# One transformer layer with experts: the last expert tile kept on chip and added with a marking matrix, the row array cleared during attention, tile 18 finished before tile 19 starts

## The chip, the core and the metric

The kernel runs on one core of one Trainium2 chip. The metric is the device time of one execution in microseconds (us); lower is better. PE is the matrix engine (TensorE), DVE is VectorE, ACT is ScalarE, POOL is GpSimd, and SP only issues transfers (DMAs). These engines run independently and wait for one another by semaphores. PE writes its results into PSUM, 8 banks of 128 x 512 float32; the rest of the on-chip data lies in SBUF.

## What is computed

A hybrid attention part adds to the residual x (1024 tokens of width 1024, all float32). The part that matters here is what follows it: each token picks one group of experts, and two experts in that group. The results of the two experts are weighted and added.

```python
top_v, top_i = lax.top_k(e_logits, EXPERT_TOPK)          # two experts of a token
top_w = jax.nn.softmax(top_v, axis=-1) * p_g
gates = jnp.sum(jax.nn.one_hot(eid, N_EXPERTS) * top_w[..., None], axis=1)
for e in range(N_EXPERTS):
    hid = jax.nn.silu(jnp.dot(h, w_gate[e])) * jnp.dot(h, w_up[e])
    y = y + gates[:, e:e + 1] * jnp.dot(hid, w_down[e])
x = x + gate_m[:, None] * y
return rms_norm(x, g_final)
```

## The kernel before

**Expert tiles.** Each of the 2048 (token, choice) pairs gets a slot in one of 20 tiles (NSTEP) of 128 slots. A tile is made of four chunks of 32 slots; a chunk belongs to one expert. The weights of the 32 experts stream through six on-chip places (the ring: gate and up projection together, and down projection), 3 MB for each expert. The loads are issued by SP in the order of use, each as soon as PE has finished with the place.

**Work on a tile n.** POOL gathers the 128 rows of the tile from DRAM (`gather`); PE transposes them (`turn_rows`), ACT and DVE copy them out with a scale and shift (`ev_t`); PE multiplies with gate and up weights (`gate_up`); ACT takes the sigmoid (`ev_sg`), DVE forms the hidden values (`ev_hid`); PE transposes them (`turn_hidden`), ACT copies (`ev_h`); PE multiplies with the down weights (`down_proj`); DVE multiplies by a row gate (`ev_y`) and writes `ysb`; POOL scatters the rows of `ysb` to `y_dram` in DRAM ("expert_rows", 2048 rows: row 1024 k + token for choice k). In the PE program tile n+1's `gate_up` and tile n+2's `turn_rows` stand between `turn_hidden(n)` and `down_proj(n)`. The indices of a tile's rows are in `lst` (tokens) and `dst_rows` (rows of `y_dram`), one column for each tile.

**The tail.** The residual of token tiles 0 to 5 (`x2_dram`) is read back into `XT` when tile 17 is through (L572). When all 20 scatters have landed (`rows_out`), SP reads `y_dram` back as 16 transfers of 512 KB into `yg[t][k]`, in the order of the token tiles t = 0 to 7 (L597). The four even token tiles (`mixed`) are summed by PE in PSUM: `add_into` adds the residual with the identity matrix as the stationary operand, and then y1 and y2 with diagonal matrices of the two weights (`diag`, made by ACT). The four odd ones are summed by DVE (`combine`). For each token tile ACT squares and sums (L1000), POOL takes the power -1/2 (L635, L636), DVE scales (`finish`, L1552), SP stores (L600). The order on DVE is combine(1), finish(0), combine(3), finish(1), finish(2), combine(5), finish(3), finish(4), finish(5), combine(7), finish(6), finish(7).

**Attention.** SP's last transfers before attention are those of the router weights (L504, L505); its next ones wait until the last scores are multiplied (`qk_done`, L507). `wuk` holds a weight of the key projection; PE reads it last in the `KV` steps, counted by `kv_ps`. Later `pick` (the chosen experts, one-hot) lies in the same place. POOL selects the keys (L675 to L677) and then takes the powers for the attention output (`o_scale`).

Of the kernel before, what the change touches and what calls it, by code (L numbers as in the profile page):

```python
# [64 lines left out]
def hybrid_layer(nc, x, c, w_ada, b_ada, g_attn, w_in, g_kv, w_uk, w_uv, lam_q1, lam_k1, lam_q2, lam_k2,  # L65
# [77 lines left out]
    y_dram = nc.dram_tensor("expert_rows", [2 * S, D], F32, kind="Internal").ap()  # L143

    ctx = ExitStack()
    with ctx:
# [165 lines left out]
        out_row_in, modc_set = sem("out_row_in"), sem("modc_set")  # L312
# [61 lines left out]
        yg = [[QKV[:, D * (2 * i + k):D * (2 * i + k + 1)] for k in range(2)] for i in range(T)]  # L374
# [44 lines left out]
        x2_out, x2_back = sem("x2_out"), sem("x2_back")  # L419
# [5 lines left out]
        def uses(b):  # L425

            return len(range(b, NSTEP, 2))

# [9 lines left out]
        def _(sp):  # L438
# [66 lines left out]
            sp.dma_start(wgr[:, :, NG:NR], w_router[0].rearrange("(j p) n -> p j n", p=P)).then_inc(wgr_in, 16)  # L505
            sp.wait_ge(qk_done, NA)
# [54 lines left out]
            for n in range(NSTEP + 1):  # L561
                if n < NSTEP:
                    sp.wait_ge(gu_ps, n + 1)
                    for w in freed(n):
                        gate_up_load(sp, expert_of(w), w % RING)
# [39 lines left out]
        def _(pool):  # L605
# [64 lines left out]
            for i, t in enumerate(sel_tiles):  # L670
# [30 lines left out]
            def overflow_rows(n, i, b):  # L701
# [16 lines left out]
                pool.wait_ge(y_out[ob], i * 16 + 16 * (uses(ob) + 1))  # L718
# [21 lines left out]
            for b in range(2):  # L740
                pool.wait_ge(y_out[b], 16 * uses(b))
# [7 lines left out]
        def _(act):  # L749
# [192 lines left out]
            act.wait_ge(modc_set, 1)  # L942
# [47 lines left out]
            for t in range(T):  # L990
                if t in mixed:
                    i = mixed.index(t)
                    act.wait_ge(mix_ps, i + 1)
                    whole = PS[:, 2 * i:2 * i + 2, :].rearrange("p a n -> p (a n)")
# [9 lines left out]
        def _(dve):  # L1004
# [246 lines left out]
            for i in range(NA):  # L1251
# [11 lines left out]
                if 5 <= i < NA // 2 + 2 and i % 4 == 1:  # L1263
# [17 lines left out]
                                     op1=ALU.mult).then_inc(modc_set, 1)  # L1281
# [93 lines left out]
            def order_experts():  # L1375
# [12 lines left out]
                dve.wait_ge(tables_set, 2 * NE)  # L1388
# [7 lines left out]
            for t in range(T + 1):  # L1396
# [22 lines left out]
                if t >= 1:  # L1419
                    if t == 1:  # L1420
                        dve.wait_ge(wgr_ready, 2)
# [68 lines left out]

            def ev_y(e, b, stored):
# [18 lines left out]
            dve.wait_ge(modc_set, 1)  # L1510
# [5 lines left out]
            for n in range(NSTEP):  # L1516
# [557 lines left out]
```

## Time and profile before

| what | us |
|---|---|
| median of three runs | 1051.61 |
| lowest and highest | 1050.21, 1052.73 |
| the profiled execution | 1047.62 |
| its span, first to last instruction | 1045.8 |
| PE busy in it | 952.2 (91%) |

The profiled execution is one of its own, 4.0 us below the median. Times within a profile are counted from the start of its span. A group of the profile is one line of the program and one kind of operation; "idle before" names what ended the wait of that engine. A float32 matmul of the program stands in the profile as two records of PE, so the 24 of `add_into` are 48 records.

### The profile page before, as it was taken

To read this page: it belongs to the slowest core of one execution; us is meant where nothing else is said; L and a number is where in the kernel's file an instruction comes from. 1 tells how busy PE (TensorE), PEld (TensorE's weight loads), DVE (VectorE), ACT (ScalarE), POOL (GpSimd) and SP (SyncE) were. 2 spreads that over 40 slices of the span, in tenths; PEclk is the share of its full clock that TensorE was granted. 3 is DMA by queue.
4 is the path that set the end of the run, shared out by engine and by line. 5 is a ranking of instruction groups with operands and counts; after the bars stand their busy time and mean duration, and the time that the engine had idled before them with its cause. 6 is when DMAs were issued, how large, how long until landed. Compare 5 with 4: busy or idle time off the path is not lost.

```text
span 1045.8 us, 14947 instructions
## 1 busy us (share of the span) xinstructions
PE 952.2 (91%) x5302; PEld 513.1 (49%) x5302; DVE 595.3 (57%) x1593; ACT 403.9 (39%) x909; POOL 115.7 (11%) x218
## 2 busy tenths in 40 slices
PE   3899999999999798879999899999499999979974
PEld 2463675444449476546666545556233434323421
DVE  3479548999997687777676333456333222312217
ACT  6130236666620577767668412122121111211113
POOL 3000000000038001110000000000111111111003
PEclk9999999999999999989999999999599999999989
DMA  9996101101111000040000411166899999999979
GB/s 326 331 359 228 41 22 41 41 21 40 40 30 18 1 1 1 1 173 11 1 2 2 161 61 60 61 261 248 323 418 422 419 417 422 419 421 421 397 284 377
DMA packets 69916, 191.44 MB, mean 183 GB/s; under 512 B 10248, under 2 KB 36160, under 8 KB 57552
## 3 DMA queue, kind: packets, MB, share of 16 engines
q1 hardware_dynamic: 61856, 172.63, 43.1%
q0 software_dynamic: 5760, 16.78, 4.1%
q10 hardware_dynamic: 2224, 1.05, 0.4%
q8 instruction: 43, 0.70, 0.3%
q14 instruction: 33, 0.27, 0.1%
HBM read 172.60 MB, written 22.04 MB: 186 GB/s over the span
## 4 chain that ended last, share of the span: by engine, by line
PE 79%; DMA 6%; issue 4%; DVE 4%; ACT 3%; SPq 3%; POOL 0%; POOLq 0%; ACTq 0%; DVEq 0%
PE PS L1675 16%; PE PS L1976 12%; PE PS L1861 11%; PE PS L1778 6%; PE PS L1999 6%; PE PS L1799 4%; PE PS L1821 3%; DMA SC<-in_w_up_dram 3%; PE PS L1722 3%; PE PS L1684 3%; PE PS L1816 3%; SPq L450 2%; PE PS L1963 2%; PE PS L1699 2%; PE PS L1664 1%
## 5 line engine op out<-in xcount | busy, mean ns | idle before, releaser
L1675 PE MATMUL PS<-HT,X 128*128 128x512 f32 x384 | 168.8, 593 | 0.0
L1976 PE MATMUL PS<-QKV,HT 128*32 128x512 f32 (+2 forms) x640 | 130.4, 607 | 3.4 <-DMA SC<-in_w_up_dram 1.7
L860 ACT ACTIVATE X<-X,nmx 128x896 f32<-128x896 f32 (+7 forms) x128 | 98.6, 772 | 68.5 <-DVE nmx L1205 68.0
L1675 PEld LDWEIGHTS PS<-HT,X 128*128 128x128 f32 x384 | 72.5, 190 | 92.4 <-issue 92.2
L1861 PE MATMUL PS<-QKV,HT 128*128 128x512 f32 x256 | 115.3, 604 | 0.0
L1141 DVE TENSOR_SCALAR_CACHE_REDUCE BIAS<-SC,tk 128x384 f32<-128x384 f32 (+3 forms) x128 | 96.4, 809 | 1.1
L1487 DVE TENSOR_TENSOR HT<-PS,HT 128x256 f32<-128x256 f32 x20 | 8.5, 425 | 153.3 <-ACT HT L958 153.3
L1778 PE MATMUL PS<-QKV 64*128 64x512 f32 (+3 forms) x384 | 82.1, 533 | 10.8 <-DVE nmx L1205 10.0
L837 ACT ACTIVATE X<-SC,tk 128x896 f32<-128x896 f32 x64 | 69.6, 1087 | 43.1 <-DVE tk L1129 43.1
L1861 PEld LDWEIGHTS PS<-QKV,HT 128*128 128x128 f32 x256 | 48.0, 193 | 54.6 <-issue 54.5
L1999 PE MATMUL PS<-QKV,HT 128*32 128x512 f32 (+2 forms) x320 | 65.4, 595 | 2.2 <-DMA X<-in_w_down_dram 2.2
L1205 DVE CUSTOM_DVE_ANT_0 X<-PS,R 128x256 f32<-128x256 f32 (+7 forms) x80 | 51.0, 675 | 28.6 <-PE PS L1778 28.2
L1799 PE MATMUL PS<-ident,X 128*128 128x128 f32 x432 | 66.1, 284 | 0.0
L1976 PE MATMUL PS<-SC,HT 128*32 128x512 f32 (+2 forms) x144 | 57.8, 604 | 6.3 <-issue 6.3
L958 ACT ACTIVATE HT<-PS 128x256 f32<-128x256 f32 x20 | 7.7, 384 | 143.3 <-PE PS L1976 143.3
L1976 PEld LDWEIGHTS PS<-QKV,HT 128*32 128x32 f32 (+2 forms) x640 | 38.1, 120 | 49.0 <-issue 46.2
L1976 PE MATMUL PS<-X,HT 128*32 128x512 f32 (+2 forms) x160 | 58.4, 621 | 0.8 <-DVE HT L1506 0.8
L1205 DVE CUSTOM_DVE_ANT_0 X<-PS,SC 128x1024 f32<-128x1024 f32 (+5 forms) x48 | 42.0, 887 | 29.4 <-PE PS L1778 29.4
L1799 PEld LDWEIGHTS PS<-ident,X 128*128 128x128 f32 x432 | 48.5, 143 | 10.6 <-issue 9.1
L1816 PE MATMUL PS<-QKV,HT 128*128 128x128 f32 x288 | 41.8, 291 | 11.1 <-ACT HT L870 11.0
L1778 PEld LDWEIGHTS PS<-QKV 64*128 64x128 f32 x384 | 32.5, 189 | 39.2 <-issue 25.2
L1821 PE MATMUL PS<-QKV 128*64 128x128 f32 x576 | 46.7, 285 | 4.1 <-ACT QKV L870 2.8
(295 smaller groups left out, 1462.9 us busy)
## 6 DMA issues: line engine op xcount, KB each, us to landing
QKV<-in_w_gate_dram SPq DMA_DIRECT2D x22, 1024.0 KB, 16.4
QKV<-in_w_up_dram SPq DMA_DIRECT2D x22, 1024.0 KB, 22.9
QKV<-in_w_down_dram SPq DMA_DIRECT2D x22, 1024.0 KB, 28.2
QKV<-in_w_ada_dram SPq DMA_DIRECT2D x8, 2048.0 KB, 15.5
QKV<-in_w_ada_dram SPq DMA_DIRECT2D x8, 1024.0 KB, 12.6
X<-in_w_in_dram SPq DMA_DIRECT2D x16, 512.0 KB, 3.8
QKV<-expert_rows SPq DMA_DIRECT2D x16, 512.0 KB, 10.0
X<-in_w_gate_dram SPq DMA_DIRECT2D x5, 1024.0 KB, 16.5
```

What stands on the lines that cost most here:

```text
L837: act.activation(RL[:, n % 2, 0:w], SC[:, sc_off[t]:sc_off[t] + w], ACT.Sign, bias=tk[:, 4, i:i + 1].bitcast(F32), scale=-1.0, accum_out=c ...
L860: act.activation(sc, sc, ACT.Exp, bias=nmx[:, i % 4, m:m + 1], scale=-1.0, accum_out=rs[:, i, m:m + 1]).then_inc(exp_done, 1)
L1141: dve.tensor_scalar(BIAS[:, i % 3, 0:w], SC[:, sc_off[t]:sc_off[t] + w], thr.bitcast(F32)[:, i:i + 1], 0.0, ALU.is_lt, ALU.add, accum_out= ...
L1205: dve.tensor_tensor_reduce(sc_buf[i % 4][:, m, 0:w], PS[:, 2 * m:2 * m + 2, :].rearrange("p a n -> p (a n)")[:, BANK * n:BANK * n + w], aw ...
L1675: end = pe.matmul(PS[:, 2 * b + half, :], WS[:, b, j, :], HT[:, j, BANK * half:BANK * (half + 1)], start=(j == 0), stop=(j == KC - 1))
L1778: end = pe.matmul(PS[:, 2 * m + n + c0 // BANK, 0:c1 - c0], QKV[rows_m, q0:q0 + P], QKV[rows_m, k0 + c0:k0 + c1], start=True, stop=True)
L1799: end = pe.transpose(PS[:, 4 + g % 2, c0:c0 + P], sc_buf[i % 4][:, m, P * b:P * (b + 1)], ident[:, :])
L1816: end = pe.matmul(PS[:, 6 + h % 2, slot], turned_at(i)[:, g % 4, P * (b - b0):P * (b - b0 + 1)], vf[:, u * S + P * b:u * S + P * (b + 1)], ...
L1821: end = pe.matmul(PS[DH * m:DH * (m + 1), 6 + h % 2, slot], vd[:, b, v0:v0 + DH], turned_at(i)[:, g % 4, c0:c0 + P], start=(b == 0), stop= ...
L1861: end = pe.matmul(PS[:, n % 4, :], HT[:, k, P * (n // 2):P * (n // 2 + 1)], wo[:, k, BANK * (n % 2):BANK * (n % 2 + 1)], start=(k == 0), s ...
L1976: end = pe.matmul(PS[at, 2 + b, :], hgT[b][:, P * c_ + at.start:P * c_ + at.stop], WGU[w][:, c_, :, :], start=(c_ == 0), stop=(c_ == KC - 1))
L1999: end = pe.matmul(PS[at, 5 + h, :], hidT[b][:, P * c_ + at.start:P * c_ + at.stop], WDN[w][:, c_, BANK * h:BANK * (h + 1)], start=(c_ == 0 ...
```

## The change

- **Last tile stays on chip.** Tile 19 (LAST) is no longer scattered. DVE multiplies its PSUM result by the row gate and by the weight of each row and leaves it in SBUF (`y_last`, `ev_y_last`). The weights of the rows come from DRAM: ACT stores the two weight arrays (`w_dram`, at tile 2), DVE works out the places of the 128 rows (`find_last_rows`, at tile 4), and POOL gathers them (`w_row`).
- **Marking matrix.** `mark_last_rows` builds, for each of the 8 token tiles, a 128 x 128 matrix of zeros and ones that says which token each row of tile 19 belongs to (`belongs`). PE multiplies it with `y_last`, and so adds the rows of tile 19 into PSUM for all 8 token tiles. For this the residual of all 8 goes through PE too (`begin`). For odd token tiles DVE's `combine` starts from PSUM. The even ones get y1 and y2 by diagonal matrices, as before (`mix`).
- **Cleared array.** Rows of tile 19 are no longer written to `y_dram`, so it is zeroed once: POOL clears `wuk` after the key selection, and SP writes it 32 times (256 KB each) to `y_dram` during attention.
- **Order.** For tile 18, PE runs `down_proj(18)` ahead of `gate_up(19)`; DVE runs `ev_y(18)` ahead of `ev_hid(19)`. `rows_out` now counts 19 scatters. The places of `yg` are moved, so that the reads of token tiles 0 to 2 go where tile 18's weights were; the reads of 3 to 7 wait for tile 19's last matmul.
- The semaphore `modc_set` becomes a step of `wgr_ready`; the other counts follow.

```diff
+            sp.wait_ge(tables_set, 2 * NE + 1)
+            for r in range(2 * T):
+                for h in range(2):
+                    sp.dma_start(y_dram[P * r:P * (r + 1), BANK * h:BANK * (h + 1)],
+                                 wuk[:, :, :].rearrange("p h d -> p (h d)")).then_inc(small_in, 16)
             sp.wait_ge(qk_done, NA)
...
             sp.wait_ge(rows_out, 1)
             for t in range(T):
+                if t == 3:
+                    sp.wait_ge(dn_ps, 2 * NSTEP)
                 for k in range(2):
...
+            pool.wait_ge(kv_ps, KV)
+            pool.memset(wuk[:, :, :], 0.0).then_inc(tables_set, 1)
             for h in range(NA // 8):
                 o_scale(h)
...
-                scatter(n)
+                if n < LAST:
+                    scatter(n)
+                if n == 4:
+                    pool.wait_ge(act_in, 48)
+                    pool.indirect_dma_start(out=w_row, out_offset=None, in_=w_dram,
...
+                if n == 2:
+                    act.dma_start(w_dram.rearrange("(p k t) o -> p k (t o)", k=2, t=T), rt[:, 5:7, :]).then_inc(act_in, 16)
...
+            def mark_last_rows():
+
+                link(dve.tensor_copy(tok_last, lst[:, LAST:NSTEP]))
+                link(dve.tensor_scalar(shift, first_tok[:, 0:T], tok_last, None, ALU.subtract))
+                for t in range(T):
+                    end = dve.tensor_scalar(belongs[:, P * t:P * (t + 1)], iota_p[:, :], shift[:, t:t + 1], 0.0, ALU.add,
+                                            ALU.is_equal)
+                end.then_inc(diag_done, 1)
+
+            def ev_y_last():
+
+                dve.wait_ge(w_in, 16)
+                for h in range(2):
+                    part = slice(BANK * h, BANK * (h + 1))
+                    dve.wait_ge(dn_ps, 2 * LAST + h + 1)
+                    dve.scalar_tensor_tensor(out=y_last[:, part], in0=PS[:, 5 + h, :], scalar=w_row, in1=out_row[:, part],
+                                             op0=ALU.mult, op1=ALU.mult).then_inc(y_sb, 1)
...
             for n in range(NSTEP):
                 turn_hidden(n, n % 2)
+                if n == LAST - 1:
+                    down_proj(n, n % 2, *weights_of(n))
                 if n + 1 < NSTEP:
                     gate_up(n + 1, (n + 1) % 2, *weights_of(n + 1))
                 if n + 2 < NSTEP:
                     turn_rows(n + 2, n % 2, 16 * (n // 2 + 2))
-                down_proj(n, n % 2, *weights_of(n))
+                if n != LAST - 1:
+                    down_proj(n, n % 2, *weights_of(n))
...
+            def begin(t):
+
+                add_into(t, ident[:, :], XT[:, t, :], True, False)
+                end = add_into(t, belongs[:, P * t:P * (t + 1)], y_last, False, t not in mixed)
+                if t not in mixed:
+                    end.then_inc(mix_ps, 1)
+
+            def mix(t):
+
+                i = mixed.index(t)
+                pe.wait_ge(yg_in[t], 32)
+                add_into(t, diag[:, i, 0, :], yg[t][0], False, False)
+                add_into(t, diag[:, i, 1, :], yg[t][1], False, True).then_inc(mix_ps, 1)
+
             pe.wait_ge(x2_back, 16 * SPILLED)
-            for i, t in enumerate(mixed):
-                if i == 2:
-                    pe.wait_ge(rows_out, 1)
-                add_into(i, ident[:, :], XT[:, t, :], True, False)
-            pe.wait_ge(diag_done, 8)
-            for i, t in enumerate(mixed):
-                pe.wait_ge(yg_in[t], 32)
-                add_into(i, diag[:, i, 0, :], yg[t][0], False, False)
-                add_into(i, diag[:, i, 1, :], yg[t][1], False, True).then_inc(mix_ps, 1)
+            pe.wait_ge(y_sb, 2 * NSTEP)
+            pe.wait_ge(diag_done, 9)
+            pe.wait_ge(rows_out, 1)
+            for t in range(4):
+                begin(t)
+            mix(0)
+            mix(2)
+            pe.wait_ge(fin_done, 1)
+            begin(4)
+            pe.wait_ge(cb_done, 1)
+            begin(5)
+            mix(4)
+            pe.wait_ge(fin_done, 3)
+            begin(6)
+            pe.wait_ge(cb_done, 2)
+            begin(7)
+            mix(6)
```

PE's program at its end, before. The rows are matmuls of the program ("x8" is eight in a row); `X,ident` adds the residual, and `QKV` alone stands for y1 and y2 with the diagonals.

```order
L2037 MATMUL PS<-X,ident 128x512 x8
L2037 MATMUL PS<-QKV 128x512 x16
```

After. `QKV` is here the marking matrix with `y_last` (two for each token tile), or y1 and y2 with the diagonals (four for each even token tile).

```order
L2098 MATMUL PS<-X,ident 128x512 x2
L2098 MATMUL PS<-QKV 128x512 x2
L2098 MATMUL PS<-X,ident 128x512 x2
L2098 MATMUL PS<-QKV 128x512 x2
L2098 MATMUL PS<-X,ident 128x512 x2
L2098 MATMUL PS<-QKV 128x512 x2
L2098 MATMUL PS<-X,ident 128x512 x2
L2098 MATMUL PS<-QKV 128x512 x10
L2098 MATMUL PS<-X,ident 128x512 x2
L2098 MATMUL PS<-QKV 128x512 x2
L2098 MATMUL PS<-X,ident 128x512 x2
L2098 MATMUL PS<-QKV 128x512 x6
```

Four more rows of the same kind follow (for token tiles 6 and 7: 2, 2, 2 and 6). The 24 matmuls have become 48: 16 with the identity, 16 with the marking matrix, 16 with the diagonals.

PE's program around tile 18, before: the transposes of tile 18's hidden values (`ident,HT`), the last of `gate_up(19)` (32-row chunks with the place `SC` among them), and then `down_proj(18)` (the row of x4).

```order
L1985 MATMUL PS<-ident,HT 128x128 x2
L1976 MATMUL PS<-SC,HT 32x512
L1976 MATMUL PS<-QKV,HT 32x512 x3
...
L1976 MATMUL PS<-SC,HT 32x512
L1976 MATMUL PS<-QKV,HT 32x512 x3
L1999 MATMUL PS<-QKV,HT 128x512 x4
L1985 MATMUL PS<-ident,HT 128x128 x2
```

After:

```order
L2043 MATMUL PS<-ident,HT 128x128 x2
L2057 MATMUL PS<-QKV,HT 128x512 x4
L2034 MATMUL PS<-SC,HT 32x512
L2034 MATMUL PS<-QKV,HT 32x512 x3
...
L2034 MATMUL PS<-SC,HT 32x512
L2034 MATMUL PS<-QKV,HT 32x512 x3
L2043 MATMUL PS<-ident,HT 128x128 x2
```

`down_proj(18)` has moved from behind the whole of `gate_up(19)` to ahead of it; the transposes of tile 19's hidden values now follow `gate_up(19)` directly.

## Rows read from the trace of the kernel before

**Rows 1.** Chain that ended last, 985 us on: start us, duration us, what.
```profile
988.27 7.07 PE PS L1976 x64
995.34 3.63 PE PS L1999 x8
...
999.67 3.69 PE PS L1999 x32
...
1003.38 0.70 DVE HT L1497
...
1004.85 5.75 DMA expert_rows<-HT,dst_rows
...
1016.02 10.62 DMA QKV<-expert_rows
```

**Rows 2.** Groups by form, 1003 to 1046 us: busy us, mean ns | idle before, releaser.
```profile
L2037 PE MATMUL PS<-QKV 128*128 128x512 f32 x32 | 14.4, 599 | 2.8 <-DMA QKV<-expert_rows 2.8
L2037 PE MATMUL PS<-X,ident 128*128 128x512 f32 x16 | 9.0, 728 | 6.1 <-DMA X<-residual_rows 6.1
```

**Rows 3.** Timeline of the end: start us, us, engine, line, operation [idle before <-releaser].
```profile
1021.90 1.02 ACT L1000 ACTIVATE HT<-PS 128x1024 f32<-128x1024 f32 x1 [18.89 <-PE PS L2037]
...
1023.98 1.28 DVE L1552 SCALAR_TENSOR_TENSOR X<-PS,ss,BIAS 128x1024 f32<-128x1024 f32 x1 [2.26 <-POOL ss L636]
...
1031.80 3.70 PE L2037 MATMUL PS<-QKV 128*128 128x512 f32 x8 [1.42 <-DMA QKV<-expert_rows]
1032.34 0.19 PEld L2037 LDWEIGHTS PS<-QKV 128*128 128x128 f32 x1 [0.24 <-issue]
...
1032.77 0.19 PEld L2037 LDWEIGHTS PS<-QKV 128*128 128x128 f32 x1 [0.24 <-issue]
...
1035.54 1.02 ACT L1000 ACTIVATE HT<-PS 128x1024 f32<-128x1024 f32 x1 [1.66 <-PE PS L2037]
...
1037.02 1.39 POOL L636 TENSOR_TENSOR ss<-ss,neghalf 128x1 f32<-128x1 f32 x1
...
1041.45 1.28 DVE L1552 SCALAR_TENSOR_TENSOR X<-X,ss,BIAS 128x1024 f32<-128x1024 f32 x1 [0.93 <-POOL ss L636]
```

**Rows 4.** Load of tile 18's down weights, issued 961.4: time to landing.
```profile
L414 SPq DMA_DIRECT2D QKV<-in_w_down_dram x1: 1645/1645/1645, 961.4 to 961.4; - x1
...
DMA to landing us min/median/max: 29.2/29.2/29.2
```

**Rows 5.** Timeline at tile 18's hidden values and behind them.
```profile
987.11 0.50 PE L1985 MATMUL PS<-ident,HT 128*128 128x128 f32 x2
...
987.31 2.98 SPq L572 DMA_DIRECT2D X<-residual_rows  x6
987.65 0.38 ACT L964 ACTIVATE HT<-PS 128x256 f32<-128x256 f32 x1 [2.50 <-PE PS L1985]
...
996.27 0.42 DVE L1489 TENSOR_TENSOR HT<-HT,PS 128x256 f32<-128x256 f32 x1
...
998.81 0.39 PE L1985 MATMUL PS<-ident,HT 128*128 128x128 f32 x2
```

**Rows 6.** Start of the tail: scatter of tile 19, first residual matmul, first read.
```profile
1009.40 9.03 PE L2037 MATMUL PS<-X,ident 128*128 128x512 f32 x16 [6.09 <-DMA X<-residual_rows]
...
1010.65 9.83 SPq L597 DMA_DIRECT2D QKV<-expert_rows  x16
```

**Rows 7.** Windows: us; busy of PE, PEld, DVE, ACT, POOL; PE clock; DMA share; GB/s.
```profile
1018.00:1022.00 4.00, 4.00 (x10) 1.69 (x10) 2.57 (x2) 0.10 (x1) 0.00 (x0) 1.00 1.03 413
...
1008.00:1012.00 4.00, 2.60 (x3) 1.18 (x4) 0.00 (x0) 0.00 (x0) 0.00 (x0) 0.50 0.14 52
```

**Rows 8.** Timeline of SP and POOL in attention.
```profile
312.50 0.82 SPq L505 DMA_DIRECT2D wgr<-in_w_router_dram  x1
...
454.92 0.37 SPq L507 DMA_DIRECT2D QKV<-in_w_out_dram  x1
...
337.82 2.35 POOL L677 TENSOR_TENSOR SC<-X,R 128x1024 f32<-128x1024 f32 x1
```

More of the change, by code:

```diff
@@ L373, in hybrid_layer @@
         diag = QKV[:, 17408:18432].rearrange("p (i k n) -> p i k n", i=4, k=2)
-        yg = [[QKV[:, D * (2 * i + k):D * (2 * i + k + 1)] for k in range(2)] for i in range(T)]
+        yg_at = [18432 + 2 * D * i for i in range(3)] + [2 * D * i for i in range(T - 3)]
+        yg = [[QKV[:, a + D * k:a + D * (k + 1)] for k in range(2)] for a in yg_at]
+        LAST = NSTEP - 1
+        assert last_use[max(range(3, NE, RING))] <= LAST - 2 and last_use[max(range(4, NE, RING))] <= LAST - 1
+        assert max(last_use[w] for w in range(NE - RING)) <= LAST - 2
+        belongs, y_last = QKV[:, 12288:12288 + S], QKV[:, 13312:13312 + D]
+        w_row, d16, tok_last, shift = nmx[:, 0, 0:1], cnt[:, 0, 0:1], cnt[:, 0, 1:2], rs[:, 0:T // 2, :].rearrange("p a b -> p (a b)")
+        w_at, k_tile = (tk[:, i, 0:1].bitcast(I32) for i in range(2))
+        pair_of = lambda t: PS[:, 2 * (t % 4):2 * (t % 4) + 2, :].rearrange("p a n -> p (a n)")
+        mixed_at = {1: 1, 3: 2, 0: 3, 2: 4, 5: 5, 4: 6, 7: 7, 6: 8}
         pick = wuk[:, :, :].rearrange("p h d -> p (h d)").rearrange("p (k t e) -> p k t e", k=2, t=T)
@@ L417, in hybrid_layer @@
         passed, tables_set = sem("passed"), sem("tables_set")
-        x2_out, x2_back = sem("x2_out"), sem("x2_back")
+        x2_out, x2_back, w_in = sem("x2_out"), sem("x2_back"), sem("w_in")
         def over(b):
@@ L560, in _ @@
                     down_load(sp, expert_of(w), w)
[L561 to L565, printed above, removed]
+            for n in range(LAST):
+                sp.wait_ge(gu_ps, n + 1)
+                for w in freed(n):
+                    gate_up_load(sp, expert_of(w), w % RING)
                 if n >= 1:
@@ L1489, in ev_hid, with find_last_rows @@
                 dve.tensor_tensor(hid[b], hh, PS[:, 2 + b, DE:2 * DE], ALU.mult).then_inc(hid_done, 1)
+            def find_last_rows():
+                link(dve.tensor_scalar(k_tile, dst_rows[:, LAST:NSTEP], 7, None, ALU.arith_shift_right))
+                link(dve.tensor_scalar(d16, dst_rows[:, LAST:NSTEP], 16.0, None, ALU.mult))
+                link(dve.scalar_tensor_tensor(out=w_at, in0=k_tile, scalar=-2047.0, in1=d16, op0=ALU.mult, op1=ALU.add))
+            def mark_last_rows():
[12 more added lines that the diff above has]
+                                             op0=ALU.mult, op1=ALU.mult).then_inc(y_sb, 1)
             def ev_y(e, b, stored):
@@ L1515, in _ @@
             ev_t(1, 1)
-            for n in range(NSTEP):
-                if n + 1 < NSTEP:
-                    ev_hid(n + 1, (n + 1) % 2)
-                if n + 2 < NSTEP:
-                    ev_t(n + 2, n % 2)
+            for n in range(LAST - 1):
+                ev_hid(n + 1, (n + 1) % 2)
+                ev_t(n + 2, n % 2)
+                if n == 4:
+                    find_last_rows()
                 ev_y(n, n % 2, n // 2)
+            ev_y(LAST - 1, (LAST - 1) % 2, (LAST - 1) // 2)
+            mark_last_rows()
+            ev_hid(LAST, LAST % 2)
+            ev_y_last()
             dve.wait_ge(route_done, 2)
@@ L1530, in _ @@
                             ev_hid(2 * i + (NSTEP + b), over(b))
-                            ev_y(2 * i + (NSTEP + b), over(b), i + uses(over(b)))
-            dve.wait_ge(act_in, 48)
+                            ev_y(2 * i + (NSTEP + b), over(b), i + scattered(over(b)))
+            dve.wait_ge(act_in, 64)
             dve.wait_ge(x2_back, 16 * SPILLED)
```

39 lines of the change are left out of this document (22 added, 17 removed).

## Prediction

> **What bounds the kernel now.** I read the chain of waits first, since only what lies on it can move the end. Up to 1003.4 us it runs along PE: gate_up(19), down_proj(18), down_proj(19). Then it leaves PE: DVE evicts tile 19 (0.70 us), its scatter takes 5.75 us to land, and then the reads of `y_dram` stand on the chain [rows 1]. So the tail, from 1003.4 us to the end of the span at 1045.8, is 42.4 us long and bound by transfers: scatter, 8 MB of reads, and the last token tiles' arithmetic. The second view is the groups of the tail: PE's work in it is 16 records with the identity and 32 with the diagonals, 23.4 us in all, and before both PE waited for a DMA [rows 2]. PE was ahead of the reads: at token tile 6 it idled 1.42 us until they landed [rows 3]. The engine clock there was full, 2.4 GHz (granted 1.00 at 1018 to 1022 us), and the transfers ran at 413 GB/s with their share at 1.03, which is all they have [rows 7].
>
> What the change does to this is two things at once: it shortens the wait for the transfers, and it doubles PE's work behind it. The sum below decides which one sets the end.
>
> **Price of a matmul of the tail.** For one even token tile four matmuls of the program took 3.70 us, eight records; two successive weight loads start 0.43 us apart (1032.34 and 1032.77) [rows 3]. A matmul of the program is two records, so it costs 0.86 us once PE runs without waits. At half the clock it is twice that: the 16 records with the identity took 9.03 us where 16 x 0.43 = 6.9 would do [rows 2, 6].
>
> **Part 1, more matmuls.** Before: 8 with the identity and 16 with diagonals, 24. After: 8 x 2 with the identity, 8 x 2 with the marking matrix, and the same 16, in all 48. 48 x 0.86 = 41.3 us, against 20.6 before. None of it can start before `y_last` is in SBUF, since PE waits for `y_sb`, `x2_back`, `diag_done` and `rows_out` ahead of the very first of them. The DVE work it replaces is nothing: `combine` still has its two operations of 1.28 us for each odd token tile, one now reading PSUM.
>
> **Part 2, when it can start.** In the new order down_proj(18) follows turn_hidden(18), which ends at 987.6, and its copy by ACT (0.38 us) [rows 5]. But its weights were issued at 961.4 and took 29.2 us, so they land at 990.6 [rows 4]. Nothing in the change speeds the weight stream. PE thus idles until 990.6, where before it did gate_up(19) from 988.3 [rows 1]. Then: down_proj(18) 3.6 us to 994.2; gate_up(19) 7.07 to 1001.3 [rows 1]. Behind it the sigmoid and the two products of DVE are no longer covered by down_proj(18): before, they ran from 995.34 to 996.69, 1.35 us [rows 1, 5], so 1002.6. From the transposes (998.81) to the start of down_proj(19) (999.67) 0.86 us [rows 1, 5], so 1003.5; down_proj(19) 3.69, 1007.2; DVE's product 0.70 [rows 1], `y_last` at 1007.9. Before, tile 19 was in SBUF at 1004.1: 3.8 us later now. On the other side, scatter 18 can start at about 995.7 instead of after 999.7, and `rows_out` falls at about 1004, 6.6 us before its old time of 1010.6, a scatter taking 5.75 us alone [rows 1], and some 8 under full load.
>
> The other thing PE waits for is the residual: its six transfers were issued at 987.3 and released PE at 1009.40 [rows 5, 6]. They keep their place. The scatter of tile 19 drops out of their company and the reads of y stand behind them on the same queue, so they may land a little earlier. The start is therefore between 1007.9 (`y_last`) and 1009.4 (as before); I take 1008.6, the middle, since nothing puts it nearer one end.
>
> **Part 3, stalls inside PE's 48.** begin(0) to begin(3) take 13.8 us, to 1022.4; the reads of token tile 0 are long there by then. mix(0) ends at 1025.8, mix(2) at 1029.3. begin(4) waits for finish(0) (it reuses its banks). From PE's end to the end of finish(0) before it was 1021.9 to 1025.3, 3.4 us [rows 3], up to 4.2 with the slower power of 1.39 us; mix(2) covers 3.4 of it. I take 0.7 us (0.2 to 1.3). The later waits (combine(1), finish(2), combine(3)) are over before PE gets to them: from mix(2) on, PE has begin(4), begin(5), mix(4) to do, 10.3 us, while DVE needs about 5.
>
> PE's end: 1008.6 + 41.3 + 0.7 = 1050.6, against 1035.5 before [rows 3].
>
> **Part 4, from PE's end to the end.** For token tile 6 before: ACT from 1035.54, POOL's power ended at 1038.4 (1037.02 + 1.39), 2.9 us [rows 3]. Then finish(6) 1.28 and finish(7) 1.28, and from the end of the last finish at 1042.73 to the end of the span 3.07 us [rows 3]. In all 8.5; 0.8 less if the power is quick. combine(7) starts from begin(7), which ends 3.4 us before PE's end, and takes 2.6: it is covered, barely.
>
> **Sum.** 1050.6 + 8.5 = 1059.1 us of span against 1045.8: +13.3 us. The span and the 1.8 us around it make up the profiled 1047.62; the median of the runs is 1051.61, so I forecast 1051.6 + 13.3 = 1064.9 us.
>
> **The reads stop being the limit.** They now start at about 1004 for token tiles 0 to 2 and at 1007.2 for the rest, on engines that are still finishing the residual. 8 MB at 413 GB/s are 20.3 us [rows 7]; with the residual in front, they end at about 1030. Tile 6 would be there at 1027, and PE asks for it at 1047. So the 4 to 5 us that the transfers gain are hidden behind PE.
>
> **Edits in the middle of the program.** The clearing: 32 transfers of 256 KB, 8 MB, about 20 us at 413 GB/s. SP has nothing to do from 313.3 to 454.9 us, and POOL ends its selection at 340.2 [rows 8], so the 32 lie at about 341 to 365, with 90 us to spare. What they can cost is that PE, DVE and ACT read SBUF beside them; in the tail the engines' durations did not grow with the transfers at 413 GB/s [rows 3, 7]. 0, at most 1.5 us. POOL's clearing of `wuk` delays the first `o_scale` by under 1 us, which waits for ACT anyway. ACT's issue at tile 2, DVE's three small operations and POOL's extra gather at tile 4 fall where DVE and POOL idle; 0, at most 0.5. The 10 operations of `mark_last_rows` lie between ev_y(18) (995.0) and the sigmoid of tile 19 (1001.7), under gate_up(19): 0.
>
> **A rule of the Trainium skill against my price.** The trace has 0.43 us for a record of 512 columns, in every stretch without waits [rows 3]. The Trainium skill, TensorE: Matmul & The Clock Gate, section Back-to-back issue gap, gives about 131 ns as the sustained spacing of 512-column matmuls in a real kernel and 216 ns as that of an isolated one, and FP8 and Floating Point Precision, section TensorE Precision Notes, says that true float32 takes four passes. By the first figure 48 matmuls would be an estimated 48 x 4 x 0.131 = 25.2 us, and the end would come at 1008.6 + 25.2 + 8.5 = 1042.3: faster than before by 3.5 us. By the second, four passes are 0.86 us, and the trace agrees with this one.
>
> **Rivals.**
> (a) *The reads stay the limit, and the change gains.* For it: the scatter's 5.75 us leave the chain [rows 1]. It needs PE's 48 to take less than about 27 us, 0.56 us each, where the row says 0.86. Then the end follows token tile 6's data, 4 to 5 us earlier: 1047.1. Against it: rows 3. Chance 0.04.
> (b) *The clock falls at the start of the tail.* After 6.09 us of idling PE ran at 1.2 GHz (granted 0.50 at 1008 to 1012) [rows 6, 7]. Now PE idles about 2.8 us at 988 to 990.6, some 1.5 at 1001.3 and 1.4 before the first of the 48. If one of these is enough, 4 us at half the clock cost 2 us; two of them 4: 1067 to 1069. For it: three gaps in 20 us. Against: PE's gap of 1.42 us ahead of token tile 6 left its pitch at 0.43 [rows 3], and the tail had fallen only after 6.09; none of these rows shows a gap of 2.8. Chance 0.08.
> (c) *The clearing disturbs attention.* If the wave of writes slows PE's and DVE's accesses for 20 us by a tenth to a fifth, 2 to 4 us: 1067 to 1069. Chance 0.03.
> (d) *The costs cancel.* PE's work begins before `y_last` is ready or part of it is off the chain. The waits stand ahead of the first matmul, so I see no way. Within 0.2% (2.1 us): chance 0.02.
>
> **How the numbers follow.** Forecast +13.3 us, 1064.9, chance 0.83. Its bounds: start -0.7/+0.8; stalls -0.5/+0.6; power -0.8/0; edits in the middle 0/+2; the median itself -1.4/+1.1 from the lowest and highest run. Added up, 1061.5 to 1069; (b) and (c) lie in its upper part. A measurement can tell about 0.2%. Faster: 0.04 (rival a). Same: 0.02. Slower: 0.94.
>
> **What the profile after would show.** Right: PE busy without a gap for about 41 us from 1008 to 1009 us on, with 96 records in `add_into`; no wait of PE for reads of y; down_proj(18) waiting for its weights until about 990.6; `y_last` at about 1008; the chain of waits on PE almost to the end. Wrong: a pitch of `add_into`'s records well under 0.43 us, a start before 1007, or PE waiting for y1 and y2.

## The result, and the profile after

Six runs of the changed kernel have a median of 1063.49 us (1060.49 to 1069.6), six of the kernel before on the same chip 1050.95 us (1049.29 to 1054.06). The ratio is 1.0123, with a 95% interval of 1.0099 to 1.0146: the change costs about 12.5 us. The profiled execution took 1063.07 us, its span is 1061.2.

The chain that ended last, in its last 55 us. Columns as in [rows 1].

```profile
990.51 2.15 issue
992.66 5.16 PE PS L2057 x8
997.82 7.05 PE PS L2034 x64
...
1007.22 3.69 PE PS L2057 x32
...
1010.92 0.76 DVE QKV L1542
1011.69 0.09 issue
1011.78 20.84 PE PS L2098 x48
1032.62 0.02 issue
1032.64 20.88 PE PS L2098 x48
...
1053.55 1.12 ACT HT L1029 x2
...
1054.75 0.20 POOL ss L655
...
1055.02 0.55 POOL ss L656
...
1055.59 2.53 DVE X L1610 x2
```

In [rows 1] the chain left PE at 1003.38 us and went through DVE, the scatter and the reads. Now it goes through DVE for one operation of 0.76 us (`y_last`) and is back on PE for 41.7 us. No DMA stands behind 1011.78 us on it. L2098 is `add_into`, 96 records in two pieces that touch.

The groups of the same stretch by form, beside [rows 2]:

```profile
L2098 PE MATMUL PS<-QKV 128*128 128x512 f32 x64 | 28.8, 592 | 0.0
...
L2098 PE MATMUL PS<-X,ident 128*128 128x512 f32 x32 | 15.2, 598 | 0.9 <-DVE QKV L1542 0.9
```

The 32 records that read from `QKV` have become 64, the 16 with the identity 32, and the two waits of PE on DMAs in [rows 2] (2.8 and 6.1 us) are gone. One wait of 0.9 us is left, on the DVE operation that writes `y_last`.

Windows of the tail, columns as in [rows 7]:

```profile
1012.00:1030.00 18.00, 18.00 (x43) 7.96 (x43) 2.57 (x2) 0.78 (x1) 0.00 (x0) 1.00 1.02 402
1030.00:1053.00 23.00, 22.98 (x55) 9.87 (x53) 15.02 (x12) 6.01 (x12) 5.27 (x12) 1.00 0.38 152
```

PE is busy for the whole of both. The transfers still run at 402 GB/s in the first, and at 152 in the second, where only stores and the last reads are left: the resource that set the end before now stands idle for much of it. So the change took the scatter and the reads off the chain, as it says, and put twice the matmuls on it.

### The profile page after: what moved, and what is told of

Read it like the earlier page. It is cut to its first block, busy times and chain, and to the rows that moved or that the text cites. A ratio compares the mean times of both kernels' runs of the same rounds, so it can differ in the third digit from the quotient of the medians.

```text
span 1061.2 us, 15094 instructions
## 1 busy us (share of the span) xinstructions
PE 974.9 (92%) x5350; PEld 522.5 (49%) x5350; DVE 597.9 (56%) x1606; ACT 403.8 (38%) x909; POOL 112.7 (11%) x219
## 4 chain that ended last, share of the span: by engine, by line
PE 82%; DMA 5%; issue 4%; ACT 3%; DVE 3%; SPq 3%; POOL 0%; DVEq 0%; ACTq 0%; POOLq 0%
PE PS L1733 16%; PE PS L2034 12%; PE PS L1919 11%; PE PS L1836 6%; PE PS L2057 6%; PE PS L1857 4%; PE PS L2098 4%; PE PS L1879 3%; PE PS L1780 3%; DMA SC<-in_w_up_dram 3%; PE PS L1742 3%; PE PS L1874 3%; SPq L464 2%; PE PS L2021 2%; PE PS L1757 2%
## 5 line engine op out<-in xcount | busy, mean ns | idle before, releaser
L2034 PE MATMUL PS<-QKV,HT 128*32 128x512 f32 (+2 forms) x640 | 131.3, 611 | 3.2 <-ACT HT L978 1.7
L2057 PE MATMUL PS<-QKV,HT 128*32 128x512 f32 (+2 forms) x320 | 66.9, 600 | 4.4 <-issue 2.6
```

Source lines behind the costliest of these rows:

```text
L2034: end = pe.matmul(PS[at, 2 + b, :], hgT[b][:, P * c_ + at.start:P * c_ + at.stop], WGU[w][:, c_, :, :], start=(c_ == 0), stop=(c_ == KC - 1))
L2057: end = pe.matmul(PS[at, 5 + h, :], hidT[b][:, P * c_ + at.start:P * c_ + at.stop], WDN[w][:, c_, BANK * h:BANK * (h + 1)], start=(c_ == 0 ...
```

## The experiments

Each run below is one kernel beside the kernel before on the same chip. Runs of one kernel scatter by some 5 us around their median, so for a comparison of two profiles I also use a shorter measure, called the tail from here on (it begins some 16 us before the prediction's tail): from SP's issue of the six residual reads to the end of the span. What happened earlier in the program drops out of it. It is 58.5 us before (issued at 987.31 [rows 5], span 1045.8) and 71.4 after (989.77, 1061.2). Its start is this line of the timeline, first of after, then of e1:

```profile
989.77 2.87 SPq L590 DMA_DIRECT2D X<-residual_rows  x6
```

```profile
991.52 2.93 SPq L590 DMA_DIRECT2D X<-residual_rows  x6
```

**e1_no_mark: what the marking matmuls cost.** Tile 19's rows are left out of the result; nothing else changes.

```diff
             def begin(t):
-                add_into(t, ident[:, :], XT[:, t, :], True, False)
-                end = add_into(t, belongs[:, P * t:P * (t + 1)], y_last, False, t not in mixed)
+                end = add_into(t, ident[:, :], XT[:, t, :], True, t not in mixed)
```

> The changed kernel without the 16 matmuls of the marking matrix (the rows of tile 19 are left out of the sum). Theory (PE's 48 matmuls of the tail set the end): 16 x 0.86 = 13.7 us off PE's tail, no new limit before that, since the reads of y end at 1033 and PE's end falls from 1053.5 to about 1040. So 13 to 14 us faster than the changed kernel, about -1 us against the kernel before (ratio 0.998 to 1.000). Rival (the reads of y or the late y_last set the end): under 2 us off, ratio 1.010 or more.

Measured: 1050.08 us, ratio 0.9995 (0.9973 to 1.0018), tail 57.7. From its chain:

```profile
1013.55 13.97 PE PS L2098 x32
...
1027.54 14.02 PE PS L2098 x32
```

32 matmuls of the program in 27.99 us, 0.87 each, where after has 48 in 41.72. The 16 marking matmuls are worth 13.7 us of tail and 13.4 us by the medians; 16 x 0.86 is 13.8. Without them the kernel is level with the one before, and the price of the prediction holds.

**e2_old_order: what the new order of tile 18 is worth.** PE and DVE take tile 18 in the order of before; the rest of the change stays.

```diff
             for n in range(NSTEP):
                 turn_hidden(n, n % 2)
-                if n == LAST - 1:
-                    down_proj(n, n % 2, *weights_of(n))
                 if n + 1 < NSTEP:
                     gate_up(n + 1, (n + 1) % 2, *weights_of(n + 1))
...
-                if n != LAST - 1:
-                    down_proj(n, n % 2, *weights_of(n))
+                down_proj(n, n % 2, *weights_of(n))
```

> The changed kernel with tile 18 in the old order (gate_up(19) ahead of down_proj(18)). Theory: y_last comes some 4 to 6 us earlier (no wait for tile 18's weights, no half clock behind it), rows_out some 2 us later; PE's 48 then start when the residual and rows_out are there, at 1009 to 1010 instead of 1011.8, and end that much earlier: 1 to 3 us faster than the changed kernel, ratio to before 1.009 to 1.011. Rival (the new order is what lets the reads start early and pays for itself): 1 to 3 us slower than the changed kernel, ratio 1.013 to 1.015.

Measured: 1066.37 us, ratio 1.0132 (1.0104 to 1.0161), tail 73.4. My theory was wrong here. I had expected 1 to 3 us less than after, since PE no longer idles for tile 18's weights; the profile has 2 us more. Its chain and its windows (columns as in [rows 7]):

```profile
1005.62 8.62 DMA expert_rows<-HT,dst_rows
...
1014.46 23.03 PE PS L2094 x48
```

```profile
1008.00:1014.00 6.00, 0.46 (x8) 0.00 (x0) 0.75 (x1) 0.15 (x1) 0.00 (x0) 0.84 0.46 175
1014.00:1018.00 4.00, 3.54 (x4) 1.51 (x5) 0.00 (x0) 0.00 (x0) 0.00 (x0) 0.50 0.67 228
```

PE had two things to wait for ahead of its first matmul of the tail, and they came together. The scatter of tile 18 starts at 1005.62, takes 8.62 us and lands at 1014.25. The last of the residual reads, issued at 995.2, lands 19.1 us later, at 1014.3, and PE's weight load names it as what it waited for:

```profile
1014.42 0.50 PEld L2094 LDWEIGHTS PS<-X,ident 128*128 128x128 f32 x2 [6.88 <-DMA X<-residual_rows]
```

Counted from the issue of the residual reads, PE starts 21.8 us later in e2 and 22.0 us later in after: no later and no earlier. What differs is what PE did just before. In e2 it was done with down_proj(19) at 1008.5, idled 6.0 us and then ran at 1.2 GHz (granted 0.50), so that the first 48 records take 23.03 us instead of 20.84. Those 2.2 us are the difference of the tails. In after, PE's own work reaches to 1010.9 and only 0.9 us of idling are left. So what failed in my theory is the start at 1009 to 1010: it took the residual to be there by then, and the last of it lands 21.6 us after the issue of the first. An earlier scatter alone would not have helped against that; e7 has this case. By the medians the two orders can't be told apart (the intervals of after and of e2 overlap); the profiles say 2 us.

**e3_clear_only: what the clearing costs.** The kernel before, with the clearing of `y_dram` during attention and nothing else of the change.

```diff
+            sp.wait_ge(tables_set, 2 * NE + 1)
+            for r in range(2 * T):
+                for h in range(2):
+                    sp.dma_start(y_dram[P * r:P * (r + 1), BANK * h:BANK * (h + 1)],
+                                 wuk[:, :, :].rearrange("p h d -> p (h d)")).then_inc(small_in, 16)
             sp.wait_ge(qk_done, NA)
...
+            pool.wait_ge(kv_ps, KV)
+            pool.memset(wuk[:, :, :], 0.0).then_inc(tables_set, 1)
```

> The kernel before with the clearing alone (POOL's memset, 32 transfers of 256 KB during attention, and their waits). Theory: between the end of the selection and POOL's next step the changed kernel's profile is 0.8 us later than that of before, so the clearing costs 0.5 to 1 us, ratio 1.0005 to 1.001. Rival (the clearing is a large part of the loss, or costs nothing): 2 to 4 us, ratio 1.002 to 1.004, or 0.

Measured: 1049.05 us, ratio 0.9982 (0.9965 to 0.9999), tail 58.6. I had put its cost at 0.5 to 1 us from one profile of after, in which POOL's work behind the selection was 0.8 us late. Over the runs it costs nothing that can be measured. That it gains 1.6 us is not shown either: the interval all but touches 1, and I have no mechanism. The traces show more directly that it costs nothing. Here are 24 us of attention, first of e3, in which the writes run, then of before, in which hardly anything is transferred (columns as in [rows 7]):

```profile
341.00:365.00 24.00, 18.33 (x100) 10.70 (x99) 17.58 (x32) 13.76 (x25) 0.59 (x2) 0.93 0.92 351
```

```profile
341.00:365.00 24.00, 18.44 (x100) 10.73 (x100) 17.80 (x32) 13.97 (x25) 0.59 (x2) 0.93 0.00 1
```

PE has the same 100 records in both and is busy for 18.33 us beside 351 GB/s of writes and for 18.44 us without them; DVE and ACT are no busier either. Rival (c) is excluded: it wanted 2 to 4 us.

**e4_odd_dve: take the residual of the odd token tiles off PE.** DVE adds it, in one more operation for each odd tile; PE has 40 matmuls instead of 48.

```diff
             def begin(t):
-                add_into(t, ident[:, :], XT[:, t, :], True, False)
-                end = add_into(t, belongs[:, P * t:P * (t + 1)], y_last, False, t not in mixed)
+                if t in mixed:
+                    add_into(t, ident[:, :], XT[:, t, :], True, False)
+                end = add_into(t, belongs[:, P * t:P * (t + 1)], y_last, t not in mixed, t not in mixed)
```

> The changed kernel in which DVE, not PE, adds the residual of the odd token tiles: 8 of PE's 48 matmuls go, DVE gets four additions of 1.3 us. Theory: 8 x 0.86 = 6.9 us faster than the changed kernel, ratio to before 1.005 to 1.0065; PE busy in add_into for 34.4 us. Rival (DVE is near its limit in the tail too): the four additions land on the path and take back 5 us, ratio 1.010.

Measured: 1060.13 us, ratio 1.0081 (1.0050 to 1.0112), tail 68.6. The 40 took 34.85 us, 6.9 less than the 48, just the 8 x 0.86. But the time fell by 2.8 us in the tail and 4.4 by the ratios. The end of the chain is as in after (7.7 us from PE's last matmul to the end of the span), so the rival, DVE at its limit, isn't what took it. The chain shows where the rest went:

```profile
994.67 6.43 PE PS L2058 x8
...
1010.51 5.30 PE PS L2058 x32
```

down_proj(18) takes 6.43 us where [rows 1] has 3.63, and down_proj(19) 5.30 where it has 3.69. Both stand behind an idle stretch of PE: 3.65 us ahead of down_proj(18), and 1.42 and 0.47 us around the transposes ahead of down_proj(19). Against after, the idle stretch is 1.1 us longer and the two down_proj are 1.3 and 1.6 us longer, 4.0 of the 4.1 us that are missing. This was the first sign that the idle time ahead of tile 18's weights costs more than itself, and it is tested in e9.

**e5_floor24: do early reads gain if PE's work doesn't grow?** As after, but without the marking matmuls and without the residual of the odd tiles on PE: 24 matmuls, as before. Tile 19's rows are left out of the result.

```diff
             def begin(t):
-                add_into(t, ident[:, :], XT[:, t, :], True, False)
-                end = add_into(t, belongs[:, P * t:P * (t + 1)], y_last, False, t not in mixed)
-                if t not in mixed:
-                    end.then_inc(mix_ps, 1)
+                end = None
+                if t in mixed:
+                    add_into(t, ident[:, :], XT[:, t, :], True, False)
```

> The changed kernel with neither the marking matmuls nor the residual matmuls of the odd token tiles: PE has the 24 matmuls of before, the reads start as early as in the changed kernel (the rows of tile 19 are left out of the sum). Measured from the issue of the residual reads to the end of the span, the kernel before took 58.5 us and the changed one 71.4. Theory: the reads, which end 43 us after that issue instead of 47, set the end again: 54.5 to 56 us, 2.5 to 4 us faster than before (ratio 0.996 to 0.998). Rival (the earlier reads bring nothing, since stores, DVE or the clock take it back): 58 us or more, ratio 1.000.

Measured: 1047.44 us, ratio 0.9965 (0.9946 to 0.9984), tail 52.7. The group of y1 and y2, and the chain:

```profile
L2097 PE MATMUL PS<-QKV 128*128 128x512 f32 x32 | 14.6, 600 | 1.8 <-DMA QKV<-expert_rows 1.8
```

```profile
1011.55 11.75 DMA QKV<-expert_rows
...
1023.34 8.90 PE PS L2097 x20
```

Here PE waits for the reads again, and they stand on the chain. The tail is 5.8 us shorter than before, near the 4 to 5 us that rival (a) gave the reads. So the idea behind rival (a) is real: it is worth 3.7 us by the ratio, and it is what the 24 added matmuls (20.6 us) buried.

**e6_best: the whole work with less of it on PE.** The residual of the odd tiles is added by DVE (as in e4). `y_last` is split into two bf16 parts, the rounded value and what is left over, and the marking matrix is bf16, so that a marking step is two bf16 matmuls and not one of float32. The residual of token tiles 0 and 2 goes through PE ahead of the waits for `rows_out` and `y_last`.

```diff
-        belongs, y_last = QKV[:, 12288:12288 + S], QKV[:, 13312:13312 + D]
+        belongs, y_last = QKV[:, 12288:12800].bitcast(BF16), QKV[:, 13312:13312 + D]
+        y_parts = [QKV[:, 14336 + 512 * i:14848 + 512 * i].bitcast(BF16) for i in range(2)]
...
+            def mark(t, start=True, stop=True):
+
+                at = belongs[:, P * t:P * (t + 1)]
+                for i, y in enumerate(y_parts):
+                    end = add_into(t, at, y, start and i == 0, stop and i == 1)
+                return end
...
+            residual(0)
+            residual(2)
+            pe.wait_ge(rows_out, 1)
             pe.wait_ge(y_sb, 2 * NSTEP)
+            pe.wait_ge(y_split, 4 + 1)
             pe.wait_ge(diag_done, 9)
```

> A complete kernel from the changed one: DVE adds PSUM to the residual of the odd token tiles (8 matmuls less); y_last is split into two bf16 parts and the marking matrix is bf16, so marking a half tile takes two cheap matmuls instead of one of float32; PE starts the residual of tiles 0 and 2 as soon as it has landed; the pairs of banks are shared so that no matmul waits for a finish. Theory (PE's time in the tail is what the change cost): 24 float32 matmuls of 0.86 and 32 bf16 ones of 0.22 us are 27.5 us instead of 41.3; tail from the issue of the residual reads 55 to 57 us instead of 71.4, ratio to before 0.996 to 0.999. Rival (a bf16 matmul of 512 columns costs as much as one record of float32, 0.43): 34 us of PE, ratio 1.002 to 1.004.

Measured: 1049.97 us, ratio 0.9999 (0.9977 to 1.0020), tail 60.6. The group of the marking matmuls, the chain, and two windows (columns as in [rows 7]):

```profile
L2116 PE MATMUL PS<-QKV 128*128 128x512 bf16 x32 | 7.6, 379 | 0.0
```

```profile
990.52 6.53 PE PS L2075 x8
...
1006.45 5.34 PE PS L2075 x32
1011.79 27.72 PE PS L2116 x80
```

```profile
989.00:996.00 7.00, 5.48 (x7) 2.41 (x8) 0.69 (x1) 0.00 (x0) 0.64 (x1) 0.53 1.00 399
...
1006.00:1010.00 4.00, 3.55 (x20) 0.98 (x24) 0.00 (x0) 2.83 (x9) 0.00 (x0) 0.57 0.78 291
```

PE's work in the tail is 27.7 us, as worked out: the 32 bf16 records are busy for 7.6 us, where 16 float32 matmuls were 13.8. The time missed its forecast by 1 to 4 us, and the windows say why: 0.53 of the clock granted behind the idle stretch at 988 to 990.5, and 0.57 at 1006 to 1010. Against [rows 1] down_proj(18) and (19) lose 2.9 and 1.7 us, and PE comes to the tail at 1011.79 although the residual was there at about 1007.8. The price of a bf16 matmul of 512 columns is as forecast too: (27.72 - 48 x 0.43) / 32 is 0.22 us.

**e7_best_old_order: e6 with tile 18 in the old order.** The edit is the one of e2, on e6.

```diff
-                if n == LAST - 1:
-                    down_proj(n, n % 2, *weights_of(n))
                 if n + 1 < NSTEP:
                     gate_up(n + 1, (n + 1) % 2, *weights_of(n + 1))
```

> As e6_best, with tile 18 in the order of before. Here PE's first residual matmuls no longer wait for rows_out, so the idle gap of 6 us of e2_old_order is filled in part. Theory: rows_out and the reads come 2 to 4 us later than in e6_best; the reads set the end, so 1 to 3 us slower than e6_best. Rival (the idling of PE at tile 18 and the half clock behind it are the larger loss): 1 to 2 us faster than e6_best.

Measured: 1051.90 us, ratio 1.0007 (0.9989 to 1.0024), tail 60.1. Between e6 and e7 neither the medians nor the tails decide: the idle time and the slow clock are only in another place.

```profile
994.59 19.28 DMA X<-residual_rows
1013.91 30.02 PE PS L2112 x80
```

PE waits for the residual to 1013.91 us, and the same 80 records then take 30.02 us instead of 27.72. Here the first matmuls don't wait for the scatter, and still PE idles 5.86 us and starts 21.7 us after the issue of the residual reads, as in e2. So in the old order it is the residual that holds PE back, with the scatter or without it.

**e8_best_f32: e6 with float32 marks.** One marking matmul of float32 in the place of two of bf16.

```diff
-        belongs, y_last = QKV[:, 12288:12800].bitcast(BF16), QKV[:, 13312:13312 + D]
+        belongs, y_last = QKV[:, 12288:12288 + S], QKV[:, 13312:13312 + D]
...
-                for i, y in enumerate(y_parts):
-                    end = add_into(t, at, y, start and i == 0, stop and i == 1)
+                for i, y in enumerate([y_last]):
+                    end = add_into(t, at, y, start and i == 0, stop and i == 0)
```

> As e6_best with the marking matmuls in float32 as in the changed kernel: 40 matmuls of 0.86, 34.4 us. Theory: 6.9 us more than e6_best, ratio 1.003 to 1.006; tail 61 to 63 us. Rival (the type of the marking matmuls is not what matters): within 2 us of e6_best.

Measured: 1055.38 us, ratio 1.0046 (1.0018 to 1.0074), tail 66.7. The chain again has one piece for all of it, 34.54 us:

```profile
1011.28 34.54 PE PS L2110 x80
```

Against e6 that is 6.8 us more of PE and 6.1 more of tail, and PE starts in both 24.5 us after the issue of the residual reads (e8 also saves DVE the splitting, which isn't on the chain). The tail is longer than the 61 to 63 us that I expected, as e6's was longer than its 55 to 57. With the same start, the tail goes nearly one to one with PE's work. Each bf16 pair saved 0.43 us of the 0.86 of a float32 matmul.

**e9_warm: does the idle stretch cost the clock?** As after, with four unused matmuls into a free bank: three between turn_hidden(18) and down_proj(18), one ahead of turn_hidden(19). They do no work of the kernel.

```diff
             for n in range(NSTEP):
+                if n == LAST:
+                    warm(1)
                 turn_hidden(n, n % 2)
                 if n == LAST - 1:
+                    warm(3)
                     down_proj(n, n % 2, *weights_of(n))
```

> The changed kernel with four matmuls whose result nobody reads: three while PE waits for tile 18's down weights, one while ACT and DVE form tile 19's hidden values. Theory (the idling of 2.6 to 3.7 us at tile 18 drops the clock behind it; in the profiles of the changed kernel, e4_odd_dve and e6_best it was 3.4 to 10.2 us at half speed, 1.6 to 4.6 us lost): down_proj(18) takes 3.6 us instead of 5.2 to 6.5, and the kernel is 1 to 4 us faster than the changed one, ratio to before 1.0085 to 1.0115. Rival (the clock there is chance and costs nothing on average, or the extra matmuls delay the chain): within 1 us of the changed kernel, 1.012, or slower.

Measured: 1062.58 us, ratio 1.0099 (1.0074 to 1.0124), tail 70.0. Of its profile, the chain and a window; below them the window of after (both with the columns of [rows 7]):

```profile
992.96 2.58 PE PS L2069 x6
...
995.68 3.67 PE PS L2057 x8
...
1008.75 3.69 PE PS L2057 x32
```

```profile
989.00:1012.00 23.00, 22.02 (x148) 7.08 (x146) 8.04 (x22) 5.01 (x15) 1.95 (x2) 1.00 0.87 347
```

```profile
992.00:996.00 4.00, 3.34 (x5) 1.56 (x6) 0.00 (x0) 0.00 (x0) 0.16 (x1) 0.57 1.01 401
```

With the unused matmuls in the place of the idle time (2.58 us of them) the clock stays at 2.4 GHz from 989 to 1012 us, and down_proj(18) takes 3.67 us instead of 5.16. The tail is 1.4 us shorter than in after, as the 1.5 us of down_proj(18) ask for. The ratios go the same way (1.0123 and 1.0099) with intervals that overlap, so the times alone don't show a gain of the kernel. What the profiles show is the clock: with the stretch left open it fell in five of five (after, e1, e4, e6 and e8, 2.58 to 3.65 us of idling), and with the stretch filled it stayed in two of two (this one and e10).

This doesn't show that the length of the gap decides. In the profile of e5 the gap at tile 18 is only 1.73 us and down_proj(18) takes 3.69 us. But the same profile has a gap of 3.13 us at 918 to 921 us, longer than that of after, and no fall of the clock in it or behind it:

```profile
921.02 0.63 PE L2056 MATMUL PS<-QKV,HT 128*32 128x512 f32 x3 [3.13 <-DMA X<-in_w_down_dram]
```

```profile
918.00:922.00 4.00, 0.98 (x12) 0.46 (x16) 1.43 (x5) 1.43 (x4) 1.02 (x1) 1.00 1.01 422
```

**e10_best2: e6 with the idle stretch filled.** The residual of token tile 6, which never leaves the chip, is useful work that can be done there; one unused matmul stands beside it, and one ahead of turn_hidden(19). The pairs of PSUM banks are shared in another order for it.

```diff
+                if n == LAST:
+                    warm(1)
                 turn_hidden(n, n % 2)
                 if n == LAST - 1:
+                    pe.wait_ge(t_sb, 2 * NSTEP)
+                    residual(6)
+                    warm(1)
                     down_proj(n, n % 2, *weights_of(n))
...
             pe.wait_ge(x2_back, 16 * SPILLED)
             residual(0)
-            residual(2)
             pe.wait_ge(rows_out, 1)
```

> e6_best, and in the gap at tile 18 PE adds the residual of token tile 6, which never left the chip, into two banks that are free by then, with one matmul whose result nobody reads; one more such ahead of tile 19's hidden values. Theory: 1.7 us of e6_best's 27.7 go into the gap, and 2 to 5 us of half clock go: tail from the issue of the residual reads 54 to 57 us instead of 60.6 (before 58.5, e5_floor24 52.6), 1 to 4 us faster than before, ratio 0.996 to 0.999. Rival (the clock is not what e6_best lost): 59 us or more, ratio 1.000.

Measured: 1048.55 us, ratio 0.9966 (0.9950 to 0.9983), tail 55.3. The fill, the window behind it, and the chain:

```profile
993.58 1.02 PE L2098 MATMUL PS<-BIAS,ident 128*128 128x512 f32 x2
...
994.78 3.67 PE L2075 MATMUL PS<-QKV,HT 128*128 128x512 f32 x8 [0.17 <-issue]
```

```profile
989.00:1012.00 23.00, 21.48 (x143) 6.78 (x132) 8.37 (x23) 4.17 (x13) 1.95 (x2) 1.00 0.88 349
```

```profile
994.00 18.14 DMA X<-residual_rows
...
1012.19 22.64 PE PS L2087 x68
```

PE idles 0.17 us ahead of down_proj(18), the clock is full throughout, down_proj(18) is back at 3.67 us, and the tail is 3.2 us shorter than before and 5.3 shorter than e6. The last 8 records of PE no longer stand on the chain: behind the 68 it goes on through ACT, POOL and DVE. The kernel does all of the computation and beats both kernels: 0.34% below the kernel before, a small gain, but with an interval clear of 1, and by the two ratios (0.9966 and 1.0123) some 1.5% below the changed one. Against e6 (0.9999) the intervals just overlap; there it is the tails that differ.

## Why the prediction was right

The forecast was slower by 13.3 us and 1064.9 us in all; 12.5 us and 1063.49 us were measured. Point by point, in the profile of after:

- **Price of a matmul: right.** 96 records in 41.72 us, 0.87 us for each matmul of the program, against 48 x 0.86 = 41.3. e1 (16 fewer: 13.7), e4 (8 fewer: 6.9) and e8 show it three more times. Here the trace also decided against the page's figure: the Trainium skill (TensorE: Matmul & The Clock Gate, Back-to-back issue gap) gives 131 ns as the sustained spacing of 512-column matmuls, and the estimate from it was 25.2 us and a gain.
- **No read in PE's way: right.** By the timeline of after, SP issued the first reads at 1006.59 us, 4.1 us earlier than in [rows 6] and, counted from the issue of the residual reads, 6.5 us earlier, where I had 6.6. PE had no wait behind its first matmul. e5 shows what they were worth when PE's work is left at 24: 5.8 us of tail.

```profile
1006.59 5.39 SPq L617 DMA_DIRECT2D QKV<-expert_rows  x8
```

- **Start of PE's work: 3.2 us off,** 1011.78 instead of the 1008.6 of part 2. Three things lie in it. 2.5 us were there before the tail: the residual reads were issued at 989.77 instead of 987.31. That is scatter of the program's earlier parts as far as I can see (the granted clock at 447 to 458 and at 587 to 598 us was 0.69 in this profile and 0.84 in the one of before), since e3 puts the clearing at no cost. 1.5 us are down_proj(18), which took 5.16 us where I had 3.6. The last 0.7 us go the other way, from the middle that I took between `y_last` and the residual: `y_last` came last.
- **The idle wait for tile 18's weights: nearly right in size, wrong in what it brings.** I had 2.6 us, counted from the end of ACT's copy, which is 3.0 us from PE's transposes on; the chain has 2.15 us from ACT's copy, and PE's idle time was 2.58. That the weights end it is seen in e6, where they land at 990.4 us and down_proj(18) starts at 990.52. But I left the clock behind it at full, and gave rival (b) a chance of 0.08. The step that failed is the sentence that PE's 1.42 us gap in [rows 3] left the pitch at 0.43: it showed what that gap did and nothing of a longer one. Rival (b) came partly true: one of its three gaps was followed by half the clock in after (1.5 us), two in e4 and e6. With 2 us a gap it had the price about right and the chance too low. In after, the weight loads of down_proj(18) show the step:

```profile
994.50 0.33 PEld L2057 LDWEIGHTS PS<-QKV,HT 128*128 128x128 f32 x1 [0.52 <-issue]
995.36 0.33 PEld L2057 LDWEIGHTS PS<-QKV,HT 128*128 128x128 f32 x1 [0.52 <-issue]
995.94 0.19 PEld L2057 LDWEIGHTS PS<-QKV,HT 128*128 128x128 f32 x1 [0.25 <-issue]
996.37 0.19 PEld L2057 LDWEIGHTS PS<-QKV,HT 128*128 128x128 f32 x1 [0.24 <-issue]
```

They are 0.86 us apart at 994.50 and 0.43 from 995.94 on: 1.2 GHz, and then 2.4.
- **Stalls inside the 48: too high.** I took 0.7 us for begin(4)'s wait on finish(0); the two pieces of the chain touch (0.02 us between them) and 41.72 us leave no room for it.
- **From PE's end to the end: 7.7 us instead of 8.5.** POOL's power took 0.55 us and not 1.39, the case that part 4 named as "quick". combine(7) was covered.
- **Edits in the middle: 0, as taken.** e3 bounds the clearing. `mark_last_rows` (1.70 us of DVE from 998.91) lies under gate_up(19).
- **Sum.** In the span: start +3.2, matmuls +0.4, stalls -0.7, end -0.8, so 2.1 over the 1059.1; the span was 1061.2. That the difference agrees within 1 us (13.3 and 12.5) and the total within 1.4 is partly chance. Two errors cancel: the 1.5 us of half clock that I left out, and the 1.5 us too much in the stalls and at the end. And the profiled execution of before lay 4 us below its median and that of after 0.4 below, so that the spans differ by 15.4 us and the medians by 12.5. The tails differ by 12.9, which is the difference that the sum was about.

What stays open: whether the old or the new order of tile 18 is better on top of e6 (e7); how the gain of e10 over e6 is shared between the clock, the moved residual and the new sharing of PSUM banks; and what, beside the length of a gap, decides whether the clock falls.

## What to carry to other kernels

Before work is moved from a transfer to an engine, price it on that engine at its real pitch and count the operations of the whole stretch, not those of the part that waits: here 5.8 us of waiting were bought off with 20.6 us of matmuls.
- **The scatter of 128 rows took 5.75, 7.48 and 8.62 us** ([rows 1], e5, e2). The first was not alone on the queues either: the last residual read landed and released PE at 1009.4 us [rows 6], 1.2 us before the scatter did. What makes the difference is not shown.
- **8 MB of writes during attention cost nothing measurable** (ratio 0.9982, 0.9965 to 0.9999), although PE, DVE and ACT were at work beside them: PE was busy for 18.33 us over 100 records with the writes and for 18.44 us over 100 without.
